# Twelve modulation chunks of a second layer computed during the first layer's feed-forward

## The chip, the cores and the metric

The kernel runs on one core of a Trainium2 chip. A core has engines that run side by side, each with its own instruction queue in program order: TensorE (PE, matrix products; PEld is its weight load), VectorE (DVE), ScalarE (ACT), GpSimd (POOL), and SyncE (SP), which here issues DMA transfers from HBM to the on-chip memory (SBUF). They wait for each other by semaphores. The metric is the device time of one execution in microseconds (us), lower is better.

## The reference

A sequence of 256 tokens of width 1024 goes through a first block of two layers and a second block of two others. The change touches the first block alone. Cut to what matters:

```
c_act = silu(c)                                   # one vector of 1024 for the whole sequence
h = layer_norm(x)
for l in range(2):
    ada = c_act @ w_ada[l] + b_ada[l]             # 6 x 1024 numbers, the "modulation"
    sh1, sc1, g1, sh2, sc2, g2 = split(ada, 6)
    u = h * (1 + sc1) + sh1
    y = mixer(u, ...)                             # mLSTM branch, dilated attention, gates, w_out
    h = layer_norm(ALPHA * h + g1 * y, ...)
    u = h * (1 + sc2) + sh2
    y = (silu(u @ w1[l]) * (u @ w3[l])) @ w2[l]   # feed-forward, inner width 2816
    h = layer_norm(ALPHA * h + g2 * y, ...)
```

The modulation depends on `c` and the weights only, so that of layer 1 can be computed at any time before its use. All is float32.

## The kernel before, in words

Every large weight is cut into chunks of 128 partitions x 2048 floats (1 MB). A list, `PLAN1`, made by `plan_first` for each layer, holds all steps of the block in order, such as ("w1", 3) or ("att", 5); each engine walks it and does its part of each step. `CHUNKS1` are the steps of the plan that load a chunk, in plan order, and that is the order in which SyncE loads them. `MAIN1` are those among them that PE multiplies; the others, "ada" and "ada_next", are modulation chunks.

A chunk goes this way. SyncE loads it into one of RING = 3 buffers `raw`; it waits until the chunk three places before is no longer needed (`await_raw`: for a main chunk until DVE has subtracted, for a modulation chunk until its result is written). For a main chunk ScalarE rounds `raw` to `w_hi` and DVE subtracts, `w_lo = raw - w_hi`, half a chunk at a time, so that PE can form a float32 product in three passes (hi x hi, hi x lo, lo x hi; 48 matmuls a chunk, L427). There are SPLIT = 2 buffers for `w_hi` and `w_lo`: a half of chunk n is rounded when PE has used the same half of chunk n-2. (Where tokens and not channels come out, as in "v" and "av", PE frees both halves at its end.) Both engines do so when they come to main step n-2 of the plan (`due`), ahead of their other work for that step.

A modulation chunk is no matrix product on PE: on DVE two multiply-and-sum instructions with `c_act` (`modulate`, L811) leave two columns in `dots`, and a small add with the bias writes them to `mod` (or to `mod1`, for the 16 columns sh1 and sc1 of the next layer, "ada_next"). In `rest_weights` DVE does those that stand between main chunks n-1 and n in `CHUNKS1` just before it subtracts chunk n. So a modulation chunk costs DVE time, a load and a turn in the ring of three.

Layer l has 24 "ada" chunks, numbers 0 to 23. The first 8 (sh1, sc1) are done ahead of the layer. Numbers 8 to 15 were taken between the steps of the mLSTM, 16 to 19 in the attention, and 20 to 23 (g2) in the layer's feed-forward, in both layers alike. The feed-forward of layer 0 also takes the 8 of "ada_next". It runs in iterations i: w1_i, w3_i, w2_(i-1), modulation chunks, with 11 of each weight. DVE forms hf = silu(.) x (.), ScalarE rounds it to hid_hi, DVE subtracts to hid_lo for w2; in iteration 0 DVE also rebuilds the residual h (step ("h", 1), L833 and L835).

In the mLSTM each of 4 heads has three steps on PE: ml_scores (L541, L544), ml_norm (L552), ml_values (L561), with DVE work between (W, the reciprocal nrm L941), and projections of other chunks set between them as cover.

Of the kernel before, what the change touches and what calls it, by code (L numbers as in the profile page):

```python
# [31 lines left out]
KT = D // P  # L32
DEPTH = 2
# [4 lines left out]
FP = FT // 2  # L38
# [48 lines left out]
def interleave(cover, steps):  # L87

    out, done = [], 0
    for n, c in enumerate(cover):  # L90
        out.append(c)
        want = (n + 1) * len(steps) // len(cover)
        out += steps[done:want]
        done = want
    return out


COUNT1 = {"u": 2, "h": 2, "qk": 8, "qk_silu": 8, "gate": 1, "gate_rows": 1, "v": 4, "aq": 6, "ak": 6, "av": 6, "ada": 3 * KT, "ada_next": KT,
          "ml_scores": MH, "ml_norm": MH, "ml_values": MH, "ml_mean": 1, "ml_var": 1, "o": 4, "gbr": 8,
          "att": 2 * SLOTS + VALUES, "wa": 4, "wb": 2, "wo": 4, "ln": 2, "w1": FP, "w3": FP, "w2": FP}  # L100


def plan_first():

    ada = [("ada", i) for i in range(KT, 3 * KT)]
    ml = [(s, h) for h in range(MH) for s in ("ml_scores", "ml_norm", "ml_values")]
    ml += [("ml_mean", 0), ("ml_var", 0)]
    att = [("att", i) for i in range(2 * SLOTS + VALUES)]
    late = [("o", i) for i in range(4)] + [("gbr", i) for i in range(8)]
    qkv = [(k, i) for k in ("aq", "ak", "av") for i in range(6)]  # L110
    plain = [("v", i) for i in range(4)] + qkv[:4]
    plan = [("u", 0)]
    for i in range(8):
        plan += [("qk", i)] + [("h", 0), ("gate", 0)] * (i == 0) + [("gate_rows", 0)] * (i == 1) + [plain[i], ("qk_silu", i)]
    qkv = qkv[4:]
    plan += interleave(interleave(qkv, ml), ada[:KT])
    plan += interleave(interleave(late, att), ada[KT:3 * KT // 2])
    plan += [("wa", 0), ("wa", 1), ("wb", 0), ("wb", 1), ("wa", 2), ("wa", 3)]
    plan += [("wo", i) for i in range(4)] + [("ln", 0), ("u", 1)]
    for i in range(FP + 1):  # L120
        if i < FP:
            plan += [("w1", i), ("w3", i)] + [("h", 1)] * (i == 0)
        if i >= 1:
            plan += [("w2", i - 1)]
        if i < 4:
            plan += [ada[3 * KT // 2 + i]]
        if 2 <= i < 2 + KT:
            plan += [("ada_next", i - 2)]
    return plan + [("ln", 1)]


# [1 line left out]
MODULATION = ("ada", "ada_next")  # L133
WEIGHTED = MODULATION + ("qk", "v", "aq", "ak", "av", "o", "gbr", "wa", "wb", "wo", "w1", "w3", "w2")
ROTATING = tuple(k for k in WEIGHTED if k not in MODULATION + ("wb", "w2"))
PLAN1 = [(kind, COUNT1[kind] * l + i) for l in range(DEPTH) for kind, i in plan_first()
         if kind != "ada_next" or l + 1 < DEPTH]
CHUNKS1 = [s for s in PLAN1 if s[0] in WEIGHTED]
MAIN1 = [s for s in CHUNKS1 if s[0] not in MODULATION]
HELD1 = [("w2", FP * l + FP - 1) for l in range(DEPTH - 1)] + [("wo", 4 * l + 3) for l in range(DEPTH)]  # L140
ROTATED1 = [s for s in PLAN1 if s[0] in ROTATING]


def first_block(nc, ctx, A, hT, k):
# [155 lines left out]
    def local(step):  # L300

        kind, N = step
        return kind, N, *divmod(N, COUNT1[kind])
# [107 lines left out]
    def tensor(pe):  # L411
# [91 lines left out]

        for step in PLAN1:
            kind, N, l, i = local(step)
# [118 lines left out]
    def scalar(act):  # L624
# [22 lines left out]

        for step in PLAN1:
            kind, N, l, i = local(step)
# [141 lines left out]
    def vector(dve):  # L791
# [46 lines left out]

        for step in PLAN1:
            kind, N, l, i = local(step)  # L840
# [1504 lines left out]
```

## Times and profile before

| | |
|---|---|
| median of 3 runs | 2222.73 us (2218.28 to 2227.90) |
| the profiled execution | 2226.38 us |
| its span, first to last instruction | 2224.6 us |
| PE, PEld, DVE, ACT busy | 92%, 86%, 68%, 45% |
| mean granted TensorE clock | 0.967 of full |
| moved by DMA | 358.98 MB, 161 GB/s over the span |

The profile is of one execution. Busy time counts an engine's instructions. A row of the timeline gives start and duration in us, engine, source line, operation, result and operands, how many instructions are merged in it, and in brackets how long the engine sat idle before it and what ended that. The names are the program's, buffer numbers left out: `projected` and `mixed` are the two sets of PSUM banks. The stages of block 1 in this execution: layer 0 up to its feed-forward to 445 us, its feed-forward to 640, layer 1's mLSTM 767 to 893, its attention to 995, its feed-forward 1064 to 1255.

### The profile page before, as it was taken

The page shows a single profiled execution, that of the slowest core. Times are in us where ns is not written, and L with a number is a line of the kernel's source. Part 1 is how long each engine was busy: PE and PEld are TensorE (multiplying, and loading weights), DVE is VectorE, ACT ScalarE, POOL GpSimd, SP SyncE. Part 2 cuts the span into 40 slices and gives each one's busy share as a digit, 9 for nine tenths or more (in the row PEclk, how much of TensorE's full clock was granted, in tenths as well). Part 3 has the DMA queues.
Part 4 walks back from the last instruction along what each step waited for, and adds up shares of the span by engine and source line. Part 5 has one row for each costly group of instructions (what it writes and reads, how often), then busy time and mean ns, then how long its engine had stood idle before and what let it go on. Part 6 is the DMA issues. An engine that isn't in the chain of part 4 may idle for free.

```text
span 2224.6 us, 37066 instructions
## 1 busy us (share of the span) xinstructions
PE 2045.8 (92%) x15578; PEld 1918.0 (86%) x15578; DVE 1521.2 (68%) x2756; ACT 995.0 (45%) x1437; POOL 22.2 (1%) x36
## 2 busy tenths in 40 slices
PE   5899999999988989999999889987999989897998
PEld 4898889999988988889899778776999878687998
DVE  7887576677668876766755478765666588655665
ACT  3553454344445544553544324444444334444444
POOL 2000000000010000000000000000000000000000
PEclk8999999999999999999999999999999999899999
DMA  8455444457644554345555343221555242123552
GB/s 316 152 190 192 168 150 154 171 212 279 240 153 141 201 195 171 130 158 186 195 206 188 111 171 132 77 77 61 196 188 190 100 137 106 58 95 114 193 198 102
DMA packets 52770, 358.98 MB, mean 161 GB/s; under 512 B 5995, under 2 KB 8651, under 8 KB 9980
## 3 DMA queue, kind: packets, MB, share of 16 engines
q1 hardware_dynamic: 52412, 356.51, 44.9%
q8 instruction: 123, 2.02, 0.4%
q14 instruction: 43, 0.35, 0.0%
q10 hardware_dynamic: 192, 0.10, 0.0%
HBM read 355.41 MB, written 1.08 MB: 160 GB/s over the span
## 4 chain that ended last, share of the span: by engine, by line
PE 79%; DVE 14%; ACT 4%; issue 1%; DMA 1%; SPq 0%; ACTq 0%; DVEq 0%
PE projected L427 31%; PE projected L1414 20%; PE mixed L427 7%; PE mixed L1414 5%; DVE cacc L1794 3%; PE mixed L1589 2%; DVE w_lo L352 1%; PE mixed L1508 1%; PE mixed L501 1%; DVE nrm L941 1%; PE mixed L479 1%; PE mixed L561 1%; PE mixed L1497 1%; PE mixed L1520 1%; PE mixed L488 1%
## 5 line engine op out<-in xcount | busy, mean ns | idle before, releaser
L352 DVE TENSOR_TENSOR w_lo<-raw,w_hi 128x1024 fp32r<-128x1024 f32 x340 | 409.4, 1226 | 232.0 <-ACT w_hi L646 230.4
L646 ACT ACTIVATE w_hi<-raw 128x1024 fp32r<-128x1024 f32 x338 | 350.6, 1055 | 376.3 <-PE projected L427 310.7
L427 PE MATMUL projected<-u_hi,w_hi 128*128 128x256 f32 x1728 | 489.9, 284 | 25.5 <-DVE u_lo L852 25.5
L427 PE MATMUL projected<-u_lo,w_hi 128*128 128x256 f32 x1728 | 484.6, 280 | 0.0
L427 PE MATMUL projected<-u_hi,w_lo 128*128 128x256 f32 x1728 | 484.2, 280 | 0.0
L427 PEld LDWEIGHTS projected<-u_hi,w_hi 128*128 128x128 f32 x1728 | 329.9, 191 | 32.6 <-issue 32.1
L1352 DVE TENSOR_TENSOR w_lo<-raw,w_hi 128x1024 fp32r<-128x1024 f32 x204 | 245.9, 1223 | 153.6 <-ACT w_hi L1648 153.4
L427 PEld LDWEIGHTS projected<-u_lo,w_hi 128*128 128x128 f32 x1728 | 329.5, 191 | 0.2
L427 PEld LDWEIGHTS projected<-u_hi,w_lo 128*128 128x128 f32 x1728 | 327.8, 190 | 0.0
L1414 PE MATMUL projected<-u_hi,w_hi 128*128 128x256 f32 x992 | 282.1, 284 | 32.1 <-DVE w_lo L1352 32.1
L1648 ACT ACTIVATE w_hi<-raw 128x1024 fp32r<-128x1024 f32 x204 | 210.9, 1054 | 158.9 <-PE projected L1414 140.6
L1414 PE MATMUL projected<-u_lo,w_hi 128*128 128x256 f32 x992 | 279.7, 282 | 0.0
L1414 PE MATMUL projected<-u_hi,w_lo 128*128 128x256 f32 x992 | 279.4, 282 | 0.0
L1414 PEld LDWEIGHTS projected<-u_hi,w_hi 128*128 128x128 f32 x992 | 190.4, 192 | 38.9 <-issue 23.4
L1414 PEld LDWEIGHTS projected<-u_hi,w_lo 128*128 128x128 f32 x992 | 191.3, 193 | 0.0
L1414 PEld LDWEIGHTS projected<-u_lo,w_hi 128*128 128x128 f32 x992 | 190.2, 192 | 0.0
L427 PE MATMUL mixed<-hid_hi,w_hi 128*128 128x256 f32 x352 | 98.9, 281 | 0.0
L427 PE MATMUL mixed<-hid_lo,w_hi 128*128 128x256 f32 x352 | 98.9, 281 | 0.0
L427 PE MATMUL mixed<-hid_hi,w_lo 128*128 128x256 f32 x352 | 98.9, 281 | 0.0
L1414 PE MATMUL mixed<-hid_hi,w_hi 128*128 128x256 f32 x352 | 98.0, 278 | 0.0
L1414 PE MATMUL mixed<-hid_lo,w_hi 128*128 128x256 f32 x352 | 98.0, 278 | 0.0
L1414 PE MATMUL mixed<-hid_hi,w_lo 128*128 128x256 f32 x352 | 98.0, 278 | 0.0
(361 smaller groups left out, 4100.9 us busy)
## 6 DMA issues: line engine op xcount, KB each, us to landing
raw<-in_stream_dram SPq DMA_DIRECT2D x324, 1024.0 KB, 4.9
w_mod<-in_first_ada_dram SPq DMA_DIRECT2D x8, 1024.0 KB, 15.1
band<-bias_rows SPq DMA_DIRECT2D x1, 3072.0 KB, 14.6
x<-in_xT_dram SPq DMA_DIRECT2D x1, 1024.0 KB, 4.9
out_dram<-uf SPq DMA_DIRECT2D x4, 256.0 KB, 2.5
tri<-in_tri_dram SPq DMA_DIRECT2D x2, 384.0 KB, 4.1
c<-in_c_dram SPq DMA_DIRECT2D x1, 512.0 KB
mask<-in_mask_dram SPq DMA_DIRECT2D x1, 384.0 KB, 25.5
```

The costliest lines, as they stand in the source:

```text
L352: eng.tensor_tensor(part(w_lo, step, half), raw_half(step, half), part(w_hi, step, half).bitcast(F32), ALU.subtract).then_inc(s_lo_dve, 1)
L427: m = pe.matmul(out, a, b, start=start and n == 0, stop=stop and n == 2, **kw)
L479: m = pe.matmul(out[:, at:at + width], qt[:, f, :], keys, start=True, stop=True)
L488: m = pe.transpose(MB[2][:, b * P:(b + 1) * P], S[:, n % ABUF, b * P:(b + 1) * P], ident[:])
L501: m = pe.matmul(out, vA[:, s, f:f + AD], PT[:, b * P:(b + 1) * P], start=b == 0, stop=b == 3)
L561: m = pe.matmul(MB[0][:, half * T:(half + 1) * T], vM[:, s, f:f + P], W[:, at:at + T], start=s == 0, stop=s == 1)
L646: act.activation(part(w_hi, step, half), raw_half(step, half), ACT.Copy).then_inc(s_hi, 1)
L1352: eng.tensor_tensor(part(w_lo, step, half), raw_half(step, half), part(w_hi, step, half).bitcast(F32), ALU.subtract).then_inc(s_lo_dve, 1)
L1414: m = pe.matmul(out, a, b, start=start and n == 0, stop=stop and n == 2, **kw)
L1589: m = pe.matmul(MB[2 + h // 2 % 2][64 * (h % 2):64 * (h % 2) + 64, t0:t1], xtok[d][:, s, h * SP:(h + 1) * SP], W[:, h % ABUF, at:at + t1 - ...
L1648: act.activation(part(w_hi, CHUNKS2[n], half), raw_half(CHUNKS2[n], half), ACT.Copy).then_inc(s_hi, 1)
L1794: ins = dve.scalar_tensor_tensor(out=out[:, half, :], in0=x[:, half, tap:tap + T], scalar=column(l, weight + tap * tiles + tile + half), i ...
```

## The change

`plan_first` now knows the layer. In layer 0 nothing moves but this: behind each iteration's own modulation chunks stands one of twelve chunks of layer 1, numbers 8 to 19 (two in iteration 10). In layer 1 the mLSTM and the attention have none. Numbers 20 to 23 stay where they were in both layers. All other code is the same, and the number of instructions of each kind too. The columns of `mod` that the twelve write (g1, sh2, sc2) have been read by layer 0 by then.

```diff
-def plan_first():
+def plan_first(l):

     ada = [("ada", i) for i in range(KT, 3 * KT)]
+    early = [("ada", 3 * KT + i) for i in range(KT, 5 * KT // 2)]
...
-    plan += interleave(interleave(qkv, ml), ada[:KT])
-    plan += interleave(interleave(late, att), ada[KT:3 * KT // 2])
+    plan += interleave(interleave(qkv, ml), ada[:KT] if l == 0 else [])
+    plan += interleave(interleave(late, att), ada[KT:3 * KT // 2] if l == 0 else [])
...
         if i < 4:
             plan += [ada[3 * KT // 2 + i]]
-        if 2 <= i < 2 + KT:
+        if 2 <= i < 2 + KT and l + 1 < DEPTH:
             plan += [("ada_next", i - 2)]
+        if l + 1 < DEPTH:
+            plan += early[len(early) * i // FP:len(early) * (i + 1) // FP]
     return plan + [("ln", 1)]
...
-PLAN1 = [(kind, COUNT1[kind] * l + i) for l in range(DEPTH) for kind, i in plan_first()
-         if kind != "ada_next" or l + 1 < DEPTH]
+PLAN1 = [(kind, COUNT1[kind] * l + i) for l in range(DEPTH) for kind, i in plan_first(l)]
```

How many modulation chunks follow iterations 0 to 10 of layer 0's feed-forward: before 1, 1, 2, 2, 1, 1, 1, 1, 1, 1, 0; now 2, 2, 3, 3, 2, 2, 2, 2, 2, 2, 2.

DVE at the start of layer 0's feed-forward, before. `mod` is the end of chunk 20's modulation, the four w_lo are w1_1 and w3_1, the last two w2_0; hT is the residual h:

```order
L814 TENSOR_TENSOR mod<-dots,vec 128x2
L352 TENSOR_TENSOR w_lo<-raw,w_hi 128x1024 x4
L1093 TENSOR_TENSOR hf<-cth,projected 128x512
L1096 TENSOR_TENSOR hid_lo<-hf,hid_hi 128x512
L833 TENSOR_TENSOR cen<-cen,rstd 128x2048
L835 TENSOR_SCALAR hT<-cen,vec 128x256 x8
L352 TENSOR_TENSOR w_lo<-raw,w_hi 128x1024 x2
```

The same place now (lines are 2 higher):

```order
L816 TENSOR_TENSOR mod<-dots,vec 128x2
L813 ISA raw,dots<-raw,cact 128x1024
L813 ISA dots 128x1
L813 ISA raw,dots<-raw,cact 128x1024
L813 ISA dots 128x1
L816 TENSOR_TENSOR mod<-dots,vec 128x2
L354 TENSOR_TENSOR w_lo<-raw,w_hi 128x1024 x4
L1095 TENSOR_TENSOR hf<-cth,projected 128x512
L1098 TENSOR_TENSOR hid_lo<-hf,hid_hi 128x512
L835 TENSOR_TENSOR cen<-cen,rstd 128x2048
L837 TENSOR_SCALAR hT<-cen,vec 128x256 x8
L354 TENSOR_TENSOR w_lo<-raw,w_hi 128x1024 x2
```

A second modulation, that of chunk 8 of layer 1, stands ahead of the subtraction of w1_1.

DVE in layer 1's mLSTM, head 1, before. W is the head's weights of the scores, nrm their norm; the w_lo are of the projection chunk two places on:

```order
L934 TENSOR_TENSOR W<-W,mixed 128x256
L811 ISA raw,dots<-raw,cact 128x1024
L811 ISA dots 128x1
L811 ISA raw,dots<-raw,cact 128x1024
L811 ISA dots 128x1
L814 TENSOR_TENSOR mod<-dots,vec 128x2
L352 TENSOR_TENSOR w_lo<-raw,w_hi 128x1024 x2
L940 TENSOR_TENSOR nrm<-nrm,em 128x512
L941 RECIPROCAL nrm<-nrm 128x512
```

And now:

```order
L936 TENSOR_TENSOR W<-W,mixed 128x256
L354 TENSOR_TENSOR w_lo<-raw,w_hi 128x1024 x2
L942 TENSOR_TENSOR nrm<-nrm,em 128x512
L943 RECIPROCAL nrm<-nrm 128x512
```

The modulation between W and the subtraction is gone.

## Rows read from the trace of the kernel before

**Rows 1.** The page, busy time and share of the span by engine.

```profile
PE 2045.8 (92%) x15578; PEld 1918.0 (86%) x15578; DVE 1521.2 (68%) x2756; ACT 995.0 (45%) x1437; POOL 22.2 (1%) x36
```

**Rows 2.** Stretches: length, busy us of PE, PEld, DVE, ACT, POOL; clock, DMA.

```profile
767.00:893.00 126.00, 117.76 (x846) 108.45 (x846) 88.01 (x140) 53.71 (x78) 0.00 (x0) 0.97 0.50 182
893.00:1000.00 107.00, 102.25 (x815) 94.28 (x815) 73.47 (x206) 55.67 (x105) 0.00 (x0) 1.00 0.41 148
...
834.00:837.40 3.40, 3.40 (x13) 2.95 (x12) 2.48 (x3) 0.60 (x1) 0.00 (x0) 0.50 0.27 58
...
465.50:482.40 16.90, 16.90 (x146) 16.90 (x145) 15.96 (x23) 5.79 (x7) 0.00 (x0) 1.00 0.62 225
482.40:499.40 17.00, 17.00 (x146) 17.00 (x145) 13.45 (x19) 7.56 (x9) 0.00 (x0) 1.00 0.88 337
...
550.30:567.20 16.90, 16.90 (x146) 16.90 (x145) 11.09 (x13) 7.31 (x9) 0.00 (x0) 1.00 0.69 248
```

**Rows 3.** Timeline of PE, layer 1's mLSTM, the values product of each head.

```profile
781.04 1.99 PE L561 MATMUL mixed<-W,vM 128*128 128x256 f32 x8 [1.24 <-DVE W L946]
...
807.13 1.99 PE L561 MATMUL mixed<-W,vM 128*128 128x256 f32 x8 [2.19 <-DVE W L946]
...
833.22 3.10 PE L561 MATMUL mixed<-W,vM 128*128 128x256 f32 x8 [2.20 <-DVE W L946]
...
861.00 3.13 PE L561 MATMUL mixed<-W,vM 128*128 128x256 f32 x7 [2.62 <-DVE W L946]
```

**Rows 4.** The chain of waits, 796 to 809 us: start, us, what.

```profile
796.39 1.23 DVE raw L811
...
799.00 2.36 DVE w_lo L352 x2
...
802.00 3.36 DVE nrm L941
...
807.13 1.99 PE mixed L561 x8
```

**Rows 5.** Timeline of ScalarE, the rounding beside it.

```profile
798.21 1.06 ACT L646 ACTIVATE w_hi<-raw 128x1024 fp32r<-128x1024 f32 x1 [1.71 <-PE projected L427]
```

**Rows 6.** Timeline of DVE, behind two other modulations of layer 1.

```profile
836.36 1.23 DVE L811 CUSTOM_DVE_ANT_0 raw<-raw,cact 128x1024 f32<-128x1024 f32 x1 [0.92 <-PE mixed L561]
...
843.58 2.36 DVE L352 TENSOR_TENSOR w_lo<-raw,w_hi 128x1024 fp32r<-128x1024 f32 x2 [4.65 <-ACT w_hi L646]
...
912.63 0.62 DVE L970 TENSOR_SCALAR og<-cacc,vec 128x256 f32<-128x256 f32 x2 [0.96 <-ACT cacc L735]
```

**Rows 7.** The chain of waits, layer 0's feed-forward.

```profile
452.01 24.24 PE projected L427 x192
476.25 5.65 PE mixed L427 x48
481.90 11.31 PE projected L427 x96
493.21 5.65 PE mixed L427 x48
```

**Rows 8.** Timeline of DVE, the same feed-forward.

```profile
458.89 1.22 DVE L811 CUSTOM_DVE_ANT_0 raw<-raw,cact 128x1024 f32<-128x1024 f32 x1
...
461.49 2.36 DVE L352 TENSOR_TENSOR w_lo<-raw,w_hi 128x1024 fp32r<-128x1024 f32 x2
...
471.85 2.69 DVE L835 TENSOR_SCALAR hT<-cen,vec 128x256 f32<-128x256 f32 x8
474.56 2.36 DVE L352 TENSOR_TENSOR w_lo<-raw,w_hi 128x1024 fp32r<-128x1024 f32 x2
...
496.00 2.36 DVE L352 TENSOR_TENSOR w_lo<-raw,w_hi 128x1024 fp32r<-128x1024 f32 x2 [1.00 <-ACT w_hi L646]
```

**Rows 9.** Loads into raw, 452 to 640 us, issue and time to landing.

```profile
L373 SPq DMA_DIRECT2D raw<-in_stream_dram x45: 327/328/328, 459.0 to 636.9; - x45
...
DMA to landing us min/median/max: 4.7/5.0/7.1
```

## The prediction

> **What bounds the kernel now.** I read the busy line first. TensorE (PE) is busy 92% of the span and VectorE (DVE) 68% [rows 1], so work leaves the path only where PE stands idle, and work put on DVE costs only where PE then waits for it. Next, the table by stretches [rows 2]. In layer 1's mLSTM (767 to 893 us) PE is busy 117.8 of 126 us, in the attention behind it 102.3 of 107, and in layer 0's feed-forward 16.9 or 17.0 of every 17: no idle at all. The change takes DVE and DMA work out of the first two and puts it into the third, so the question is how much of the 8.2 us idle in the mLSTM belongs to the modulation, and what slack the feed-forward has beside a saturated PE.
>
> The four waits of PE in the mLSTM stand in [rows 3]: 1.24, 2.19, 2.20 and 2.62 us, which is the 8.2 us, each before the values product (L561) of one head and each ended by DVE's W. The chain of waits [rows 4] shows the second: a modulation's two products on DVE (raw L811, from 796.39), the two subtractions (w_lo from 799.00), the reciprocal, W, PE.
>
> **What is removed: layer 1.** One modulation chunk holds DVE for 2.60 us (458.89 to 461.49, [rows 8]). Twelve are 31.2 us of DVE time, but what they cost the path is this:
> - Heads 1 and 2: a modulation stands directly in the chain. Without it the subtraction can't start 2.6 us earlier, since its second half needs ScalarE's w_hi, which starts at 798.21, when PE has used the buffer, and takes 1.06 [rows 5]: 799.27, plus one half subtraction of 1.23 makes 800.50, against 801.36 now. Gain 0.86 each, 1.7 together. The waits become about 1.35, near the 1.24 of head 0, which has no modulation in its chain.
> - Heads 0 and 3, 3.86 us of the idle: ahead of head 3's wait DVE itself sat idle until ScalarE's w_hi, as the row at 843.58 shows for such a chunk (4.65 us idle, after the modulation at 836.36) [rows 6]. Gain 0.
> - Attention: behind the modulation at 906.7 DVE ends its subtraction and is still 0.96 us early for ScalarE [rows 6]. Gain 0 for the four.
> - The clock. At 834.0 the granted clock falls from 1.00 to 0.50 for 3.4 us [rows 2], right behind the 2.20 us wait; the values product takes 3.10 instead of 1.99 [rows 3] and the chunk behind it another 0.3. Behind the 1.24 us wait it does not fall. I take this fall as gone: 1.4. The one behind 2.62 stays.
>
> Gain: 1.7 + 1.4 = 3.1 us; bounds 0 and all the idle of the stretch with both falls, 8.2 + 2.9 = 11.1.
>
> **What is added: layer 0's feed-forward.** One chunk is 5.65 us on PE, three make an iteration of 16.96 [rows 7]. Each iteration i orders w1_i, w3_i, w2_(i-1), modulations, w1_(i+1). There were 1, 1, 2, 2 modulations behind iterations 0 to 3 and 1 behind 4 to 9; now there are 2, 2, 3, 3, then 2. DVE is busy 15.96 of 16.9 in the stretch that holds the first w2, 13.45 with two modulations, 11.09 with one [rows 2]. One more makes 18.6, 16.0 and 13.7. The first doesn't fit; 13.7 is what two modulations cost now without a PE wait.
>
> There is a second limit. Raw chunks rotate through 3 buffers, so a chunk's load starts when the chunk three before it is released, and takes 4.9 us alone, 5 to 7 beside others [rows 9]. Behind w3_0 the chunks were ada20, w1_1; now ada20, E8, w1_1 (E8 to E19 are the twelve). So w1_1, which was long there, starts loading at 459.0. With three modulations in a row the next w1 waits for the first of the three. Worked through from the trace's times (PE needs the first half of w_lo; a half rounds in 1.0 on ScalarE and subtracts in 1.2):
> - w1_1: lands 463.9, rounded 465.0, first half of w_lo 466.2. PE wants it at 464.95 (452.01 + 24.24 less two chunks). Wait 1.25.
> - w2_0: E8's 2.6 and ScalarE's rounding of w3_1, which now waits behind w1_1's and the Silu, end the first result's hid_lo at 473.4 and the 5.0 us of h (L833 and L835) at 478.5; it was 474.54 [rows 8]. First half at 479.7, and PE is ready at 477.5: wait 2.2. The old slack here was 0.5.
> - w1_2: w2_0 done 480.9, ada21 and E9 to 486.1; its load starts at 480.9, lands 485.8, rounded 486.9, first half 488.1. PE ready at 485.35: wait 2.75.
> - w1_3: now three modulations. w1_2's second half at 489.3, hf, hid_lo, w3_2 and w2_1 to 496.1, ada22 to 498.7; the load of w1_3 starts there and lands at 504.7 (6.0, beside others); first half 507.0. PE ready at 505.1: wait 1.9.
> - w1_4: the same pattern, wait 1.95.
> - w1_5 on: two modulations, load released by w2 and not by a modulation. First half 1.1 us before PE wants it, as now (1.7 early at 496.00 + 1.2 against 498.86). No wait. The last two, E18 and E19, stand ahead of the last w2 in that pattern too.
>
> Sum of the waits: 10.05. Bounds: 0 if loads and order give the slack back, and 10 + 9 if each of the four loads that decide takes the longest seen, 7.1 and not 4.9 [rows 9].
>
> The clock again: behind waits of 1.9 to 2.75 it can fall, at 1.4 each. A fall while DVE is what is late (w2_0, w1_2) only fills the next wait. Behind w1_3 and w1_4 it is on the path; of such waits in [rows 3], 2.19 had none and 2.20 and 2.62 had one. I take one in two: 1.4.
>
> Instructions added or removed beside these: none; the twelve loads and products are the same ones. SyncE issues a load in 0.33 us [rows 9].
>
> **Sum.** -3.1 + 10.05 + 1.4 = +8.3 us. The profiled execution took 2226.4 us round a span of 2224.6 and lies 3.7 above the median of 2222.7. So the next profiled one would be 2234.7 and the median 2231.0.
>
> A word on bandwidth. An iteration with two modulations moved 5 chunks at 337 GB/s and a DMA share of 0.88 [rows 2]; 6 chunks in 16.96 us are 371 GB/s, which by that share (383 at 1.00) just fits. The Trainium skill (DMA: Bandwidth & Descriptors, Specifications) gives a core's HBM limit as about 358 GB/s: by it six chunks take 17.6 us, 0.6 more than the iteration in each of two, an estimate from that page which my waits of 1.9 already exceed. No run here shows 371 yet.
>
> **Rivals.**
> 1. *Not slower: the feed-forward absorbs it.* If w1_1's late load is covered and DVE catches up in its idle (3.5 us per iteration at 13.45 of 17), the waits are 0 to 3 us and the mLSTM's gain decides: 2222.7 - 3.1 + up to 3 = 2219.6 to 2222.6. For it: no PE idle before, DVE share 0.79. Against: the ring, and DVE's 18.6 in 16.9. The point from which it decides: hid_lo and h of the first iteration ending by 475.6, when w2_0 would be on time. Chance 0.15; beyond it, 0.03 that more than 11 us go, which needs all of the mLSTM's idle.
> 2. *The DMA decides.* Loads queue at 5 to 6 chunks per iteration, each deciding load is 2.2 longer, waits spread to iterations 4 to 9: 2231.0 + 8.8 = 2239.8. For it: loads of 6 to 7 us occur when three are under way. Against: at 0.88 share nothing waited. Chance 0.20.
> 3. *A fall of the clock behind every wait, small waits else.* 8.3 + 2.8: 2233.8. Chance 0.14.
> 4. *The change doesn't do what it says* (PE idle unchanged in both places): 2222.7. Chance 0.03.
>
> **How the numbers follow.** My forecast has 0.45. 0.5%, 11.1 us, is about what can be told from no change here. Faster by more: 0.03. Slower by more (above 2233.8): rival 2, part of rival 3, and the upper end of my own case (some 3 us off in five worked waits): 0.20 + 0.05 + 0.08 = 0.33. Same: 0.64. The range goes from rival 1's waits of 0 to rival 2, 2220 to 2241.
>
> **What would show it.** In the after profile: (a) PE's waits before L561 of layer 1 are 1.2 to 1.4 for heads 0 to 2, 2.6 for head 3, and the clock stays at 1.00 round 834; (b) the attention lasts as long as before; (c) from w1_0 to the last w2 the feed-forward is 10 to 12 us longer, all of it within its first four iterations, in waits for w_lo or for ScalarE's w_hi behind a load; (d) iterations 4 to 10 keep 16.96. Waits in (d) would make me wrong on the DMA, none in (c) on the ring.

## The result, and the profile after

The changed kernel takes 2237.41 us (median of 20 runs, 2222.8 to 2260.8), the one before 2220.43 in the same runs. The ratio is 1.0071, 95% interval 1.0050 to 1.0091: 0.7% slower, some 16 us (11 to 20). That lies in the range given (2220 to 2241), but beyond the 0.5% within which I had put 0.64 of the chance; the class it fell in had 0.33. The profiled execution took 2229.95 us (span 2228.2), only 3.6 above the one before. It is one of the shorter of the twenty, and why is told below.

The waits of PE in layer 0's feed-forward behind w1_0, of which there were none before (the 2.69 us ahead of w1_0 are in both). Timeline of PE, changed kernel; in brackets the idle time ahead of the instruction and what ended it:

```profile
466.44 0.36 PE L429 MATMUL projected<-u_hi,w_hi 128*128 128x256 f32 x1 [1.87 <-DVE w_lo L354]
...
479.67 0.36 PE L429 MATMUL mixed<-hid_hi,w_hi 128*128 128x256 f32 x1 [2.09 <-DVE w_lo L354]
...
489.06 0.45 PE L429 MATMUL projected<-u_hi,w_hi 128*128 128x256 f32 x1 [3.71 <-DVE w_lo L354]
...
510.58 0.55 PE L429 MATMUL projected<-u_hi,w_hi 128*128 128x256 f32 x1 [3.33 <-DVE w_lo L354]
...
532.42 0.36 PE L429 MATMUL projected<-u_hi,w_hi 128*128 128x256 f32 x1 [2.50 <-DVE w_lo L354]
...
650.60 0.38 PE L429 MATMUL mixed<-hid_hi,w_hi 128*128 128x256 f32 x1 [2.05 <-DVE hid_lo L1098]
```

The first five are w1_1, w2_0, w1_2, w1_3 and w1_4, the five places that were named; the sixth, the last w2, was not. Sum 15.55 us. What ended the fourth and fifth, and what the projections behind the waits took, stands in the chain of waits of the same execution (start, us, what):

```profile
480.68 5.83 DMA raw<-in_stream_dram
...
489.06 7.32 PE projected L429 x48
...
501.05 0.17 DVE mod L816
501.23 0.02 issue
501.24 6.78 DMA raw<-in_stream_dram
508.02 0.02 issue
508.05 1.06 ACT w_hi L648
...
509.21 1.24 DVE w_lo L354
510.44 0.14 issue
510.58 8.48 PE projected L429 x48
...
523.91 5.96 DMA raw<-in_stream_dram
...
532.42 12.77 PE projected L429 x96
545.18 5.44 PE mixed L429 x48
550.62 10.88 PE projected L429 x96
```

At 501.05 the first of three modulations is written, and that releases the buffer into which w1_3 is then loaded; load, rounding and subtraction follow one another, and PE waits for all. A chunk takes 7.32 and 8.48 us where 5.44 is the pace at the end of the fence: the clock had fallen.

```profile
489.00:492.60 3.60, 3.54 (x17) 3.57 (x18) 2.58 (x4) 1.92 (x3) 0.00 (x0) 0.53 0.69 225
509.60:516.50 6.90, 5.92 (x28) 5.95 (x29) 5.62 (x6) 3.34 (x5) 0.00 (x0) 0.51 0.59 218
```

(Stretches as in [rows 2]; the third number from the end is the granted clock: half, 1.2 of 2.4 GHz.) The three falls cost 1.88 + 3.04 + 1.89 = 6.8 us (7.32 and 8.48 less 5.44, 12.77 less 10.88).

In layer 1's mLSTM, against [rows 3]:

```profile
800.39 1.56 PE L563 MATMUL mixed<-W,vM 128*128 128x256 f32 x6 [1.44 <-DVE W L948]
...
825.65 1.56 PE L563 MATMUL mixed<-W,vM 128*128 128x256 f32 x6 [1.36 <-DVE W L948]
...
850.91 1.56 PE L563 MATMUL mixed<-W,vM 128*128 128x256 f32 x6 [1.36 <-DVE W L948]
...
877.04 1.75 PE L563 MATMUL mixed<-W,vM 128*128 128x256 f32 x6 [2.62 <-DVE W L948]
```

2.19 and 2.20 became 1.36, and the clock did not fall at the third head. Head 0 stands 19.35 us later than before (800.39 against 781.04), head 3 only 16.04 (877.04 against 861.00): 3.3 us came back. But only 16.1 of the 19.35 are the feed-forward's; 3.2 were lost between it and head 0, where this execution has one fall of the clock more, at 786 us. So in this execution the gain only made up for that.

**Where 14 us of the profiled execution went.** A chunk of a feed-forward has two paces, both at a granted clock of 1.00: 5.65 us (48 matmuls 118 ns apart) or 5.44 us (113 ns). In [rows 7] it is 11.31 for two chunks, here it is 10.88 from 550.62 on. Before, three of the four feed-forwards of the program ran at 118 ns; after, one. With 33 chunks of 0.21 each that is 6.9 us a feed-forward, 13.9 for two. The first sum of it: 15.55 of waits + 6.8 of clock - 6.7 for the faster pace (32 chunks) = 15.6, and the feed-forward's last product ended 16.1 later (656.32 against 640.2). The second: 3.6 + 13.9 = 17.5, near the medians' 17.0; this agreement is no proof, since the paces of the executions without a profile are not known. So one profile of each understated the change, and waits, falls and pace have to be counted apart. That the pace differs by chance is how I read it; no run sets it.

### The profile page after: what moved, and what is told of

It is laid out like the page before. It is cut to its first block, busy times and chain, and to the rows that moved or that the text cites. A ratio compares the mean times of both kernels' runs of the same rounds, so it can differ in the third digit from the quotient of the medians.

```text
span 2228.2 us, 37066 instructions
## 1 busy us (share of the span) xinstructions
PE 2034.6 (91%) x15578; PEld 1907.6 (86%) x15578; DVE 1519.8 (68%) x2756; ACT 991.9 (45%) x1437; POOL 22.4 (1%) x36
## 4 chain that ended last, share of the span: by engine, by line
PE 75%; DVE 16%; ACT 5%; DMA 2%; issue 2%; SPq 0%; ACTq 0%; DVEq 0%
PE projected L429 29%; PE projected L1416 20%; PE mixed L429 6%; PE mixed L1416 5%; DVE cacc L1796 3%; DVE w_lo L354 2%; PE mixed L1591 2%; DMA raw<-in_stream_dram 1%; PE mixed L1510 1%; PE mixed L503 1%; DVE nrm L943 1%; PE mixed L481 1%; ACT w_hi L648 1%; PE mixed L563 1%; PE mixed L1499 1%
```

## The experiments

Each was timed in five rounds beside the kernel before (8 to 12 times in all), and profiled once. Since pace and falls of the clock vary, I give the ratio and PE's waits over 0.25 us in layer 0's feed-forward, from the one profile.

| kernel | ratio (95%) | PE's waits there, us |
|---|---|---|
| changed | 1.0071 (1.0050 to 1.0091) | 1.87, 2.09, 3.71, 3.33, 2.50, 2.05 = 15.6 |
| a_drop12 | 0.9985 (0.9959 to 1.0010) | 1.28 |
| a_add12 | 1.0078 (1.0052 to 1.0104) | 1.45, 1.68, 2.81, 3.06, 2.20, 1.18, 2.30 = 14.7 |
| a_load_only | 1.0074 (1.0047 to 1.0101) | 1.66, 1.69, 2.79, 2.69, 2.44, 0.98, 1.58 = 13.8 |
| a_dve_only | 1.0017 (0.9994 to 1.0039) | 1.71, 0.62, 1.79, 0.70, 0.65 = 5.5 |
| b_turn_only | 1.0075 (1.0042 to 1.0108) | 1.51, 1.67, 2.60, 1.76, 1.42, 1.62 = 10.6 |
| b_bytes_only | 1.0012 (0.9988 to 1.0035) | 2.53, 1.28 = 3.8 |
| b_spread | 1.0072 (1.0047 to 1.0096) | 1.45, 6.15, 0.30 = 7.9 |
| b_six | 0.9997 (0.9970 to 1.0024) | 1.12 |
| c_first1 | 1.0019 (0.9995 to 1.0043) | 1.87, 2.09 = 4.0 |
| c_pair23 | 1.0022 (0.9995 to 1.0049) | 1.17, 2.51, 2.76 = 6.4 |
| c_eight | 0.9996 (0.9969 to 1.0023) | 0.34, 0.82, 1.81 = 3.0 |
| c_parked12 | 1.0042 (1.0015 to 1.0069) | 0.97, 0.64, 1.72, 2.96, 2.62, 1.33 = 10.2 |

### Removal and addition apart

a_drop12, to the changed kernel:

```diff
-        if l + 1 < DEPTH:
-            plan += early[len(early) * i // FP:len(early) * (i + 1) // FP]
```

> The twelve chunks are left out altogether (the columns g1, sh2, sc2 of layer 1 keep layer 0's numbers), so this is the removal alone: layer 1 without them, layer 0's feed-forward as it was. Theory A (two modulations stand in layer 1's chain, the rest are off the path): 3 us faster than the kernel before, at most 5; waits before L563 of heads 1 and 2 at 1.35 us; the feed-forward of layer 0 without a PE wait. Theory B (taking 12 MB of loads and 31 us of VectorE out of layer 1 gives much more, and the feed-forward takes it all back): 8 us faster or more. Theory C (the difference of the two kernels is only the streaming pace of matmuls, 113 or 118 ns apart, which varies by stage from run to run): nothing but that pace differs, within 2 us of before on the median.

a_add12, to the kernel before (a kind of its own, results into a spare tile):

```diff
+    early = [("ada_extra", i) for i in range(3 * KT // 2)]
...
+        if l + 1 < DEPTH:
+            plan += early[len(early) * i // FP:len(early) * (i + 1) // FP]
```

> Layer 1 as before, and twelve more modulation chunks in layer 0's feed-forward at the places where the changed kernel has them (their results go to a spare tile and are not used): the addition alone. Theory A: the feed-forward costs 20 us more than before (five waits of 1.9 to 3.7 us, one of 2 at the end, and falls of the clock behind them), so 3 us slower than the changed kernel, 2240. Theory B: 25 us or more above before. Theory C: no more than 5 us above before.

Removal alone: 0.15% faster, 3 us, which the interval doesn't tell from nothing; the waits in the mLSTM are as expected:

```profile
796.82 1.56 PE L561 MATMUL mixed<-W,vM 128*128 128x256 f32 x6 [1.16 <-DVE W L946]
...
822.09 1.56 PE L561 MATMUL mixed<-W,vM 128*128 128x256 f32 x6 [1.37 <-DVE W L946]
```

Addition alone: 0.78%, 17 us, about the whole loss. Theory B falls: its removal should have given 8 us or more (0.9964), which is inside the interval of a_drop12, but its addition 25, which is outside of a_add12's (at most 23); and the waits of a_drop12 show no more won. Theory C, that only the pace differs, falls with a_add12. The 1.28 us in a_drop12 stands at w2_0, without any extra modulation: [rows 7] showed no wait there, but PE was there sooner now, for two reasons. This feed-forward ran at 5.44 us a chunk and not at 5.65, 0.8 us over four chunks; and before, the clock was at half for 3.4 us from 451.7, ahead of w1_0, so that its first chunk took 7.1 us, where here no such fall came and it took 6.1. In c_eight, at the same pace but with that fall, the wait for w2_0 is 0.34 us. The slack of 0.5 us that I read there was one of the slow pace and of a fall.

### Loads and VectorE time apart

a_load_only, to the changed kernel, in `modulate`:

```diff
+            if l == 1 and step in EARLY1:
+                products_left_out[0] += 2
+                dve.tensor_tensor(to[:, 2 * i:2 * i + 2], dots[:], vecs[...], ALU.add).then_inc(s_ada, 1)
+                dve.wait_ge(s_ada, n)
+                return
```

> The changed kernel, but the twelve chunks in the feed-forward are only loaded and released, their two products on VectorE left out (g1, sh2, sc2 of layer 1 are wrong). What the loads and the ring of three cost alone. Theory A (ring and VectorE together): w1_1 waits 1.2 us for its late load, w1_3 and w1_4 some 1.8 each since their load starts only when the first of three modulations is done, the last w2 about 1: 6 to 8 us over a_drop12. Theory D (HBM or the DMA engines are the bound, VectorE is not): 15 us or more over a_drop12, nearly all of the changed kernel's loss. Theory E (VectorE alone): within 2 us of a_drop12.

a_dve_only, to a_drop12, in `rest_weights` (EXTRA: one at w1_1 to w1_10 each, two at the last w2):

```diff
+                for _ in range(EXTRA.get(MAIN1[n], 0) if 1 in halves else 0):
+                    for half in range(2):
+                        w = gab[:, 4 * half:4 * half + 4, :].rearrange("p a t -> p (a t)")
+                        ins = dve.tensor_tensor_reduce(out=w, in0=w, in1=k["cact"][:], ...)
```

> No loads for the twelve, but the same two products each on VectorE at the same places in layer 0's feed-forward, on memory that is free then (results of the twelve missing). What VectorE's time costs alone. Theory A: w1_1 0.3, w2_0 1.7, w1_2 1.9, w1_3 and w1_4 some 1 us of wait each, with a fall of the clock or two 6 to 8 us over a_drop12, and nothing from iteration 4 on. Theory D: within 2 us of a_drop12. Theory E: 15 us or more over a_drop12.

With the loads alone PE waits at the same places nearly as long:

```profile
466.20 0.36 PE L429 MATMUL projected<-u_hi,w_hi 128*128 128x256 f32 x1 [1.66 <-DVE w_lo L354]
...
479.43 0.36 PE L429 MATMUL mixed<-hid_hi,w_hi 128*128 128x256 f32 x1 [1.69 <-DVE w_lo L354]
...
487.93 0.36 PE L429 MATMUL projected<-u_hi,w_hi 128*128 128x256 f32 x1 [2.79 <-DVE w_lo L354]
...
508.84 0.36 PE L429 MATMUL projected<-u_hi,w_hi 128*128 128x256 f32 x1 [2.69 <-DVE w_lo L354]
```

and the time is that of the changed kernel (1.0074). VectorE's 31 us of products without the loads cost 5.5 us of waits and a ratio of 1.0017. Theory A had both at 6 to 8 us over a_drop12. It was right for VectorE (7 us, though the two intervals overlap) and far too low for the loads (20 us); D's number for the loads held, E fell.

### The turn in the ring or the bytes

b_turn_only, to a_load_only:

```diff
-        sp.dma_start(raw[:, c % RING, :], A["stream1"][c]).then_inc(s_landed[c % RING], 16)
+        w = CHUNK // 16 if CHUNKS1[c] in early else CHUNK
+        sp.dma_start(raw[:, c % RING, 0:w], A["stream1"][c][:, 0:w]).then_inc(s_landed[c % RING], 16)
```

> As a_load_only (no products for the twelve), but each of the twelve loads brings only a sixteenth of its bytes; it still takes its turn in the ring of three and is released at the same place (g1, sh2, sc2 of layer 1 are wrong). Theory R (the turn: a modulation chunk holds one of three buffers, so the next main chunk's load starts late): 12 us or more over a_drop12, waits of PE at w1_1, w1_2, w1_3, w1_4 and the last w2 as in a_load_only, each up to 1.5 us shorter since the deciding load has less beside it. Theory H (bytes: six chunks in 17 us are more than HBM gives): no more than 5 us over a_drop12.

b_bytes_only, to a_drop12, in SyncE's loop, ahead of w1_1 to w1_10 and twice ahead of the last w2:

```diff
+            for _ in range(EXTRA.get(CHUNKS1[c], 0)):
...
+                sp.dma_start(gab[:, 8 * (n % 2):8 * (n % 2) + 8, :].rearrange("p a t -> p (a t)"),
+                             A["stream1"][c]).then_inc(s_extra[n % 2], 16)
```

> The twelve are left out of the ring and of VectorE's work, but twelve loads of 1 MB go at the same places of SyncE's queue into memory that is free in layer 0's feed-forward (g1, sh2, sc2 of layer 1 are wrong). The bytes without the turn. Theory R: no more than 5 us over a_drop12; single loads take 6 to 7 us but start early enough, no wait of PE above 1 us. Theory H: 12 us or more over a_drop12, DMA share at 0.95 or more in iterations 2 and 3 and PE waiting there.

With a sixteenth of the bytes the ratio is 1.0075, the same; with all the bytes and no turn in the ring it is 1.0012. So the turn alone, that a modulation chunk takes one of three buffers, is enough for the whole loss, as theory R has it, and the bytes alone are not. That does not make it the only cost: see c_parked12 below. And the bytes are not free in iterations 2 and 3. In b_bytes_only PE waited there and nowhere else:

```profile
504.08 0.36 PE L441 MATMUL projected<-u_hi,w_hi 128*128 128x256 f32 x1 [2.53 <-DVE w_lo L352]
...
523.55 0.36 PE L441 MATMUL projected<-u_hi,w_hi 128*128 128x256 f32 x1 [1.28 <-DVE w_lo L352]
```

and the loads into `raw` between 482 and 505 us landed later than when the twelve were only small, here the row of each (min/median/max; bytes only, then turn only, whose row has small loads among the eight that it counts):

```profile
DMA to landing us min/median/max: 4.9/7.8/8.9
```

```profile
DMA to landing us min/median/max: 2.0/5.3/8.5
```

R had expected no wait above 1 us in b_bytes_only; there it was wrong. While w1_3's load was under way there, the 16 DMA engines were busy throughout (the last two numbers are their share and GB/s):

```profile
492.60:501.60 9.00, 8.95 (x76) 8.74 (x75) 4.99 (x11) 0.05 (x1) 0.00 (x0) 1.00 1.01 424
```

So the loads that come together here share a rate that is used up for these 9 us, though over 17 us it is not.

### One or two chunks by themselves

c_first1 moves number 8 alone, c_pair23 numbers 8 and 9:

```diff
+        if l + 1 < DEPTH and i == 0:                   # c_first1
+            plan += early
```

```diff
+        if l + 1 < DEPTH and i in (2, 3):              # c_pair23
+            plan += early[i - 2:i - 1]
```

> One chunk alone is moved, number 8, into iteration 0 of layer 0's feed-forward; the other eleven stay in layer 1. All results. Theory R (as worked out in the prediction): PE waits 1.5 to 1.9 us at w1_1, whose load now starts at 459, and 1.7 to 2.1 at w2_0, since VectorE is 2.6 us and a late rounding behind; w1_2 then 0 to 1.2, with no second extra modulation ahead of it. Together 3 to 5 us of waits from one chunk, none later; 2 to 4 us over before in time. If the waits of iteration 0 need the second extra modulation too: under 1.5 us.

> Two chunks alone are moved, numbers 8 and 9, into iterations 2 and 3, where three modulations then stand in a row; ten stay in layer 1, and none of them in the chain of heads 1 and 2. All results. Theory R: w1_3 and w1_4 are each loaded only when the first of the three is done: PE waits of 1.7 to 3.3 us at each of the two and at no other place of this feed-forward, and 1.6 to 1.9 us fewer in the mLSTM: 1 to 4 us over before. If these waits in the changed kernel only came from being late out of iterations 0 and 1: under 1 us each.

c_first1 repeats the first two waits of the changed kernel to the hundredth, 3.96 us from one chunk:

```profile
468.64 0.36 PE L429 MATMUL projected<-u_hi,w_hi 128*128 128x256 f32 x1 [1.87 <-DVE w_lo L354]
...
481.86 0.36 PE L429 MATMUL mixed<-hid_hi,w_hi 128*128 128x256 f32 x1 [2.09 <-DVE w_lo L354]
```

c_pair23 shows three modulations in a row without anything late before them. Its chain of waits into w1_3:

```profile
490.00 1.23 DVE w_lo L354
491.23 1.14 DVE raw L813
...
493.56 0.17 DVE mod L816
493.74 5.96 DMA raw<-in_stream_dram
499.73 1.06 ACT w_hi L648
...
500.89 1.24 DVE w_lo L354
502.26 5.72 PE projected L429 x48
```

The first modulation (490 to 493.7) stands ahead of the load, the other two run on VectorE meanwhile and cost nothing. Both waits (2.51, 2.76) are in the expected 1.7 to 3.3. The 1.17 at w2_0, where none was expected, is the one that a_drop12 has too. The ratios of both kernels are above 1, neither clear of it.

### Other orders and other memory

b_spread puts the modulation chunks of an iteration one behind each main chunk, from iteration 1 on:

```diff
+        if i < FP:
+            plan += [("w1", i)] + own[:1] * (i > 0)
+            plan += [("w3", i)] + [("h", 1)] * (i == 0) + own[1:2] * (i > 0)
+        if i >= 1:
+            plan += [("w2", i - 1)]
+        plan += own[2:] if i else own
```

> The changed kernel, but from iteration 1 on the modulation chunks of an iteration stand one behind each main chunk (w1, w3, w2) and not in a row behind w2. Same loads, same VectorE work, all results. Theory R: no main chunk's load waits for the first of three modulations any more, so the waits at w1_3 and w1_4 go (3 us each) and those at w1_1 and w2_0 stay: 5 to 10 us faster than the changed kernel, about 2229. Theory H: within 3 us of the changed kernel. If a modulation in front of w2 or w3 delays these instead, the same waits appear there, and it is no faster.

The waits at w1_3 and w1_4 went, as expected, and that of the last w2 too. But one modulation now stood ahead of w3_1, another between h and w2_0 on VectorE, and PE waited 6.15 us for w2_0. The waits halved, 7.9 against 15.6, yet the ratio is that of the changed kernel, 1.0072. Part of it is a side effect of the edit, which has no test of the layer: in layer 1's feed-forward numbers 21 to 23 moved too, and PE waited 4.15 us for its w2_0, where the changed kernel waited 0.5.

```profile
1102.34 0.55 PE L434 MATMUL mixed<-hid_hi,w_hi 128*128 128x256 f32 x1 [4.15 <-DVE w_lo L359]
```

With it 12.1 us of waits stand against 16.1, and the 4 between them are within what the two intervals leave open. The profiled execution also had a mean granted clock of 0.961 against 0.967; what that took isn't settled.

c_parked12 computes all twelve at the same places, from two places in gab and not from the ring:

```diff
+            for _ in range(EXTRA.get(CHUNKS1[c], 0)):
...
+                if n >= 2:
+                    sp.wait_ge(s_parked, n - 1)
+                sp.dma_start(spot(n), A["parked"][n]).then_inc(s_extra[n % 2], 16)
```

> All twelve at the same places of VectorE's order as in the changed kernel, but loaded into two places of their own (in gab, which is free in layer 0's feed-forward) and not into the ring of three. All results. Theory R: the load's turn was the cost; what stays is VectorE's time, waits as in a_dve_only, 4 to 6 us in all, and the last w2 1 us. 2 to 5 us over before, 12 us less than the changed kernel. Theory H, if loads and products only cost together: 10 us or more over before.

It lost 0.42%, 9 us (3 to 15), where R had 2 to 5 and H 10 or more; the intervals of this and of the changed kernel overlap, so that taking away the turn alone is not shown to win anything. Of its 10.2 us of waits 5.6 are at w1_3 and w1_4, where b_bytes_only had 3.8 and a_dve_only 0.7. The trace says why: w1_3's load starts early, with no modulation ahead of it, but takes 8.89 us beside the others, where in b_turn_only it took 5.22.

```profile
490.81 8.89 DMA raw<-in_stream_dram
```

So the turn is enough for the loss, but without it bytes and products together still cost over half as much. The three don't add up: each hides part of the others.

b_six and c_eight take only what fits, one a iteration from 4 to 9, c_eight two more behind iteration 10:

```diff
+        if l + 1 < DEPTH and 4 <= i < 10:              # b_six
+            plan += early[i - 4:i - 3]
```

```diff
+        if l + 1 < DEPTH and 4 <= i < FP:              # c_eight
+            plan += early[i - 4:i - 3] if i < FP - 1 else early[6:]
```

> Only six chunks are moved (numbers 8 to 13 of layer 1, one behind each of iterations 4 to 9 of layer 0's feed-forward, two modulations in a row there at most); 14 to 19 stay in layer 1, none of them in the chain of heads 1 and 2. All results. Theory A with R: the mLSTM's 3.3 us are won and no wait comes in the feed-forward, 2 to 4 us faster than before, 2216 to 2218. If two in a row already cost (1.2 us was seen once at iteration 8): same as before, 2220.

> Eight chunks are moved: numbers 8 to 13 behind iterations 4 to 9, 14 and 15 behind iteration 10; 16 to 19 stay in the attention. All results. Theory R: two in a row nowhere cost PE a wait in iterations 4 to 9 (under 1 us in all), but the last w2 has no other chunk between it and w2_9, its load waits for w2_9's buffer and it waits for hid_lo behind it: 1.6 to 2.3 us there. The mLSTM's waits before L563 are 1.2 to 1.4 for heads 0 to 2. Sum: within 2 us of before.

Both are 0.7% faster than the changed kernel, by their ratios to the same kernel, and the same as before (0.9997, 0.9996). In b_six the mLSTM's two waits are 1.36 each:

```profile
805.57 1.56 PE L563 MATMUL mixed<-W,vM 128*128 128x256 f32 x6 [1.36 <-DVE W L948]
...
832.07 1.56 PE L563 MATMUL mixed<-W,vM 128*128 128x256 f32 x6 [1.36 <-DVE W L948]
```

so 2.0 us are won there (head 3's product comes 77.9 us after head 0's, before 79.96), but no kernel here is shown to beat the one before. c_eight has the wait at the last w2, 1.81 us, and b_six, which moves nothing to iteration 10, has none.

## Why the prediction was right in kind and short in size

That the range covers the measured time is in part luck: its upper end was set by rival 2, the DMA, which is not what happened. The places of the waits were worked out: the five named came, and a sixth, not named, with them. Point by point, by its own steps:

- *PE bounds, and only what it waits for counts.* Right. 31 us of VectorE work taken from layer 1 gave 3.3 within the mLSTM (predicted 3.1): two waits to 1.36 (predicted 1.35), head 3 unchanged at 2.62.
- *The clock's fall at 834 goes.* It went; but a fall of the clock also came at 786 us in the changed kernel, ahead of the mLSTM, where none had been. The same number of such falls need not appear in any one execution: in b_six, c_eight and b_turn_only one came between the products of heads 0 and 3, with waits of no more than 1.4 us there.
- *Waits in the feed-forward, 10.05 us.* The places were right, all five; the sizes were 1.87, 2.09, 3.71, 3.33, 2.50 against 1.25, 2.2, 2.75, 1.9, 1.95, together 13.5. The mis-sized term is the time of the loads that decide: 4.9 and 6.0 us were put in for w1_2 and w1_3, 5.83 and 6.78 came. And PE asks earlier at the faster pace, by 0.4 at w1_1. In a_add12, which ran 9 of the 11 chunks ahead of w1_4 at 117 to 118 ns and whose two loads took 5.13 and 6.51, the same five waits are 11.2, so some 2 of the 3.5 us may be the pace and no error of the steps. The ratios of a_load_only and a_dve_only show where the weight lies: I had treated VectorE's time and the ring as equals, and the turn in the ring alone gives all of the loss, VectorE's time alone 7 us.
- *The last w2 waits for nothing.* This step failed. I said that two modulations there stand in the pattern of iterations 4 to 9. They do in the ring, but in the others three chunks of PE lie between w3_i and w2_i, and here only w2_9. Before, w2_10's load was released by w1_10; now it starts when w2_9 has been subtracted:

```profile
640.05 4.88 DMA raw<-in_stream_dram
...
644.96 1.07 ACT w_hi L648
```

  VectorE ends the two modulations at 645.1 and idles 1.0 us more for that rounding. Only then come w2_10's subtraction and, behind it, hf and hid_lo of w3_10, for which w2_10 waits: 2.05 us at 650.60, and 1.81 again in c_eight. The load's turn decides here (a_load_only: 1.58 without the products), and the products alone would do less (a_dve_only: 0.65).
- *A fall of the clock, 1.4 us.* Short: 6.8 in the profiled execution, three falls, one of them 6.9 us long.
- *VectorE with 13.7 of 17 us in the later iterations costs nothing.* Nearly right: no wait in iterations 4 to 9 of the changed kernel, and one each of 0.98 (a_load_only), 1.18 (a_add12) and 0.82 (c_eight).
- *The signs.* (b) held: from head 3's product to w1_0 of the next feed-forward 205.6 us before, 203.9 after, with 4 us less at half clock. (c) did not: the feed-forward is 16.1 longer and not 10 to 12, and 2.05 of it lie at its end. (d) held, at the other pace: an iteration takes 10.88 + 5.44 = 16.3 us.
- *The sum.* +8.3 was forecast and 16 to 17 measured. Of the difference 3.5 are the five waits, 2.05 the last w2, 5.4 the clock, as far as one execution tells; that is 10.9 for the 8.7 to be explained, and before's own mixture of paces and falls is in the rest.
- *Rivals.* "The DMA decides" named longer loads and had 2239.8; of it the longer loads are seen, but no wait moved to iterations 4 to 9, and b_bytes_only shows that the bytes alone don't give the loss. The absorption (0.15) did not occur. As to a core's limit of about 358 GB/s that the Trainium skill gives (DMA: Bandwidth & Descriptors, Specifications): these traces go above it, so here the measurement decides. The first stretch is of the kernel before, the second of b_bytes_only:

```profile
11.90:28.90 17.00, 6.64 (x20) 4.21 (x18) 16.15 (x26) 5.01 (x6) 0.00 (x0) 0.78 1.02 423
```

```profile
482.40:499.40 17.00, 17.00 (x147) 17.00 (x146) 13.16 (x18) 5.25 (x6) 0.00 (x0) 1.00 0.88 351
```

  "No run here shows 371 yet" was thus wrong when I wrote it: the trace of the kernel before has 423 near its start. My 383 for a share of 1.00 was too low as well. At 423 GB/s six chunks take some 15 us (an estimate from that row), so they fit into an iteration of 17; the first wait of b_bytes_only comes from loads that bunch within 9 us of it.

## What to carry to other kernels

Where transfers of different use rotate through one small ring, an item that seems free on every engine still takes a turn: ask which load its release starts and when that load is needed, and move it only to places where the next urgent load doesn't hang on it. Before work is moved, ask whether its removal is on the path where it is (here 3 us of 31), for the place where it goes must then cost less than that. And check the ends of a loop by themselves, since there the distance between producer and consumer is shorter.

## What the runs showed of the hardware that I had not expected

- Two paces of the same matmul stream at a granted clock of 1.00: 113 and 118 ns from start to start, often held over a whole feed-forward, in some (a_load_only's and c_eight's first) changed within it. In the 14 profiled executions, 56 feed-forwards, 20 ended at 118. What chooses is open. It makes 7 us a feed-forward, so a single profile of this kernel is not good to better than 0.5%.
- In layer 0's feed-forward the clock fell after PE waits of 2.50 to 3.71 us in the changed kernel and not after its 1.87, 2.09 and 2.05; in [rows 3], 2.19 had none and 2.20 had one. The length of the wait does not settle it: it also stayed at 1.00 after 2.51 in c_pair23 and 2.96 in c_parked12. One of the falls stayed for 6.9 us, of which PE worked 5.9.
- A 1 MB load that takes 4.7 to 4.9 us alone took up to 8.9 in c_parked12 with others under way, and up to 10.6 in b_bytes_only.
- DMA into SBUF ran at 423 GB/s over 17 us (kernel before, 11.9 to 28.9 us) and 424 over 9 us in the middle of a feed-forward with PE busy (b_bytes_only).
